# Dilated attention on one core: the two heads of a pair alternate on opposite halves of TensorE, and the next scores stand between transposes and value products

## What is computed

```python
DILATED_GROUPS = ((128, 1), (512, 4), (2048, 16))      # window, dilation; 16 heads of 64 in each

def dilated_attention_mixer(h, w_qkv, q_gain, k_gain, w_o, rel_bias):
    qkv = (h @ w_qkv).reshape(b, s, N_ATTN_GROUPS, 3, HEADS_PER_GROUP, HEAD_DIM)
    for g, (window, dil) in enumerate(DILATED_GROUPS):
        q = head_rms_norm(qkv[:, :, g, 0], q_gain[g])
        k = head_rms_norm(qkv[:, :, g, 1], k_gain[g])
        v = qkv[:, :, g, 2]
        ...
        o, l = dilated_group_attention(q, k, v, bias_g, dil, (window // 2) // dil)
    ...

def dilated_group_attention(q, k, v, bias_g, dil, n_side):
    ...
    sc = jnp.einsum('brnqhe,brnkhe->brnhqk', qb, kb, preferred_element_type=jnp.float32) * (e ** -0.5)
    sc = jnp.where(allowed[None, None, :, None], sc + bias, -1e30)
    m = jnp.max(sc, axis=-1, keepdims=True)
    p = jnp.exp(sc - m)
    den = jnp.sum(p, axis=-1, keepdims=True)
    o = jnp.einsum('brnhqk,brnkhe->brnqhe', (p / den).astype(v.dtype), vb)
```

## Time and profile before

| | |
|---|---|
| median of 3 runs | 3167.93 us (3167.38 to 3170.23) |
| time of the profiled execution | 3171.36 us |
| its span in the trace | 3169.6 us |
| mean granted clock of TensorE | 0.95 of full speed |
| TensorE busy with matmuls | 2895.6 us, 91% |
| the attention stage's three groups, from the first values to the last product | about 1148 to 1785 us of the span |

### The profile page before, as it was taken

One profiled execution on the slowest core, in us unless ns is written; L12 is line 12 of the kernel. 1 busy time (PEld: TensorE's weight loads), 2 busy tenths in 40 slices (PEclk: granted clock), 3 DMA queues, 4 the chain that ended last, 5 costly groups with the idle time before them and its releaser, 6 DMA issues.

```text
span 3169.6 us, 39147 instructions
## 1 busy us (share of the span) xinstructions
PE 2895.6 (91%) x15958; PEld 2352.6 (74%) x15958; DVE 1562.8 (49%) x2318; ACT 1096.0 (35%) x1689; POOL 237.6 (7%) x216
## 2 busy tenths in 40 slices
PE   6999997489999989989999799999799999889877
PEld 5787886467888878768797478888688888566665
DVE  5776663834434434543424554344544343543665
ACT  4332332343222224534525332222332122532442
POOL 2333220010000000000000120000200000010000
PEclk9999998789999989989999899999899999898888
DMA  3244547433443221112231232222122222211101
GB/s 116 88 143 154 161 149 209 188 119 101 133 125 106 94 92 57 67 52 83 69 114 67 94 108 98 93 95 104 42 93 93 98 102 93 76 41 41 39 15 42
DMA packets 115140, 305.40 MB, mean 96 GB/s; under 512 B 28064, under 2 KB 73568, under 8 KB 86160
## 3 DMA queue, kind: packets, MB, share of 16 engines
q1 hardware_dynamic: 109840, 281.41, 27.0%
q10 hardware_dynamic: 5120, 21.50, 1.8%
HBM read 265.20 MB, written 41.85 MB: 97 GB/s over the span
## 4 chain that ended last, share of the span: by engine, by line
PE 80%; DVE 8%; ACT 3%; issue 2%; POOL 1%; SPq 1%; DMA 0%; DVEq 0%; ACTq 0%; POOLq 0%
PE ps L94 78%; DVE s_ L121 2%; PE ps L99 1%; SPq L158 1%; DVE H_ L121 1%; DVE htf_ L135 1%; ACT htf_ L117 1%; ACT wh_ L117 0%; ACT hh_ L117 0%; DVE wl_ L121 0%; DVE Pm_ L121 0%; ACT sq_ L117 0%; DVE ol_ L121 0%; DVE nmx_ L143 0%; DVE R_ L121 0%
## 5 line engine op out<-in xcount | busy, mean ns | idle before, releaser
L94 PE MATMUL ps<-hh_,wh_ 128*128 128x512 f32 x2184 | 874.0, 400 | 23.9 <-DVE hl_ L121 12.7
L94 PE MATMUL ps<-hl_,wh_ 128*128 128x512 f32 x2184 | 857.7, 393 | 0.0
L94 PE MATMUL ps<-hh_,wl_ 128*128 128x512 f32 x2184 | 856.7, 392 | 0.0
L121 DVE TENSOR_TENSOR wl_<-raw_,wh_ 128x2048 fp32r<-128x2048 f32 (+2 forms) x213 | 481.1, 2259 | 543.0 <-ACT wh_ L117 543.0
L117 ACT ACTIVATE wh_<-raw_ 128x2048 fp32r<-128x2048 f32 (+2 forms) x213 | 399.7, 1876 | 341.4 <-PE ps L94 324.8
L94 PEld LDWEIGHTS ps<-hh_,wh_ 128*128 128x128 f32 x2184 | 414.9, 190 | 127.5 <-DVE hl_ L121 11.4
L94 PEld LDWEIGHTS ps<-hl_,wh_ 128*128 128x128 f32 x2184 | 415.0, 190 | 87.3 <-issue 4.0
L94 PEld LDWEIGHTS ps<-hh_,wl_ 128*128 128x128 f32 x2184 | 414.2, 190 | 88.1
L94 PE MATMUL ps<-ah_,wl_ 128*128 128x512 f32 x704 | 279.5, 397 | 0.0
L94 PE MATMUL ps<-ah_,wh_ 128*128 128x512 f32 x704 | 278.3, 395 | 0.0
L94 PE MATMUL ps<-al_,wh_ 128*128 128x512 f32 x704 | 277.8, 395 | 0.0
(11 more groups left out here) (337 smaller groups left out, 3612.7 us busy)
## 6 DMA issues: line engine op xcount, KB each, us to landing
raw_<-in_w SPq DMA_DIRECT2D x205, 1024.0 KB, 4.9
sO<-s5ce_ SPq DMA_DIRECT2D x32, 256.0 KB, 4.0
sW<-s5wt_ SPq DMA_DIRECT2D x16, 512.0 KB, 3.7
sA<-os_ SPq DMA_DIRECT2D x24, 256.0 KB, 2.2
ol_<-sA SPq DMA_DIRECT2D x24, 256.0 KB, 3.9
sT<-sK SPq DMA_DIRECT2D x32, 128.0 KB, 3.3
wh_<-sO ACTq DMA_DIRECT2D x4, 1024.0 KB, 11.6
wl_<-sO ACTq DMA_DIRECT2D x4, 1024.0 KB, 13.2
```

The lines of the kernel that those rows point to most:

```text
L94: return self.e.matmul(out, lhsT, rhs, start=start, stop=stop, skip_group_check=True)
L121: return Nothing() if self.e is None else self.e.tensor_tensor(out, a, b, op)
```

## The change

In `scores_tensor` the loop over the heads becomes the innermost: for each block the matmul of head 0 (SBUF partitions 0 to 63, the upper half of the array's rows) is followed by that of head 1 (partitions 64 to 127). The banks of both heads are waited for before the first of a part. In `products_tensor` the value products alternate likewise between output partitions 0 to 63 and 64 to 127 (the two halves of the array's columns), and wait for the turned tiles of both heads. For that, `turned_parts` lists the parts of both heads next to each other. All transposes of a pair now run in one go; behind them come the scores of the next pair, and then all value products. Step 1 and step 8 keep the order of their pieces.

```diff
--- before.py
+++ after.py
@@ -1590,7 +1590,7 @@
                  (2, 0, 128, 2), (2, 128, 128, 3), (3, 0, 128, 3), (3, 128, 64, 4)]
     else:
         parts = [(x, 0, 128, x) for x in range(4)]
-    return [(h, parts[b:b + 4]) for h in range(2) for b in range(0, len(parts), 4)]
+    return [(h, parts[b:b + 4]) for b in range(0, len(parts), 4) for h in range(2)]
 
 
 def turned_number(g, c, n):
@@ -1676,18 +1676,20 @@
 def scores_tensor(K, pe, g, c):
     q, k = K.att.qk[c % 2]
     w = 256 if g == 0 else 128
-    for h in range(2):
-        r = slice(64 * h, 64 * h + 64)
-        for b0, blocks in enumerate(score_parts(g)):
-            b = K.mb.take("S", g, c, h, b0)
+    pe.wait_ge(*K.at("a.hn", g, c, 0))
+    pe.wait_ge(*K.at("a.hn", g, c, 1))
+    for b0, blocks in enumerate(score_parts(g)):
+        banks = [K.mb.take("S", g, c, h, b0) for h in range(2)]
+        for h in range(2):
             pe.wait_ge(*K.after(pe, K.mb, "S", g, c, h, b0))
-            pe.wait_ge(*K.at("a.hn", g, c, 0))
-            pe.wait_ge(*K.at("a.hn", g, c, 1))
-            for n, x in enumerate(blocks):
-                lo, hi = (max(0, 128 * x - 64), min(512, 128 * x + 192)) if g == 0 else (128 * x, 128 * x + 128)
-                o = w * n + (lo - (128 * x - 64) if g == 0 else 0)
-                m = pe.mm(b[:, o:o + hi - lo], q[r, 128 * x:128 * x + 128], k[r, lo:hi], True, True)
-            m.then_inc(*pe.up("S", g, c, h, b0))
+        for n, x in enumerate(blocks):
+            lo, hi = (max(0, 128 * x - 64), min(512, 128 * x + 192)) if g == 0 else (128 * x, 128 * x + 128)
+            o = w * n + (lo - (128 * x - 64) if g == 0 else 0)
+            for h in range(2):
+                r = slice(64 * h, 64 * h + 64)
+                m = pe.mm(banks[h][:, o:o + hi - lo], q[r, 128 * x:128 * x + 128], k[r, lo:hi], True, True)
+                if x == blocks[-1]:
+                    m.then_inc(*pe.up("S", g, c, h, b0))
     pe.mark("a.S", g, c)
 
 
@@ -1744,7 +1746,7 @@
         ac.mark("a.P", g, c, h)
 
 
-def products_tensor(K, pe, g, c):
+def products_tensor(K, pe, g, c, scores=None):
     A = K.att
     i = c % 2
     O = K.gb.take("O", g, c)
@@ -1752,14 +1754,16 @@
     todo = turned_parts(g)
 
     def weigh(n):
-        h, sub = todo[n]
         t = turned_number(g, c, n)
         pe.wait_ge(*K.at("a.PT", t))
-        hd = 2 * c + h
-        for y, (x, c0, nk, vt) in enumerate(sub):
-            m = pe.mm(O[64 * h:64 * h + 64, 128 * x:128 * x + 128], A.V[0:nk, vt, 64 * hd:64 * hd + 64],
-                      A.PT[t % 4][0:nk, 128 * y:128 * y + 128], g != 0 or y % 2 == 0, g != 0 or y % 2 == 1)
-        m.then_inc(*pe.up("a.w", t))
+        pe.wait_ge(*K.at("a.PT", t + 1))
+        for y, (x, c0, nk, vt) in enumerate(todo[n][1]):
+            for h in range(2):
+                hd = 2 * c + h
+                m = pe.mm(O[64 * h:64 * h + 64, 128 * x:128 * x + 128], A.V[0:nk, vt, 64 * hd:64 * hd + 64],
+                          A.PT[(t + h) % 4][0:nk, 128 * y:128 * y + 128], g != 0 or y % 2 == 0, g != 0 or y % 2 == 1)
+                if y == 3:
+                    m.then_inc(*pe.up("a.w", t + h))
 
     if c == 0:
         for j in (-2, -1):
@@ -1774,10 +1778,10 @@
         m.then_inc(*pe.up("T", t))
         if n == 1 and c + 2 < 8:
             head_tensor(K, pe, g, c + 2, 1)
-        if n > 1:
-            weigh(n - 2)
     pe.mark("a.T", g, c)
-    for n in range(max(0, len(todo) - 2), len(todo)):
+    if scores is not None:
+        scores_tensor(K, pe, g, scores)
+    for n in range(0, len(todo), 2):
         weigh(n)
     pe.mark("O", g, c)
 
@@ -1838,11 +1842,11 @@
             if c == 8:
                 scores_tensor(K, pe, g, 7)
             if c > 1:
-                products_tensor(K, pe, g, c - 2)
+                products_tensor(K, pe, g, c - 2, c - 1 if c < 8 else None)
             if c < 2:
                 head_tensor(K, pe, g, c, 1)
-            if 0 < c < 8:
-                scores_tensor(K, pe, g, c - 1)
+            if c == 1:
+                scores_tensor(K, pe, g, 0)
     pe.mark("end", "pe", "attend")
 
 
```

## The result

| | before | after |
|---|---|---|
| median | 3167.89 us of 4 runs (3167.38 to 3170.23) | 3133.68 us of 4 runs (3130.6 to 3134.51) |
| ratio, with its 95% interval | | 0.9889 (0.9872 to 0.9906) |
| span of the profiled execution | 3169.6 us | 3132.4 us |

The change saves 34.2 us; 3133 was forecast, with 3125 to 3146 as the range. The page of the kernel after still gives most of the chain that ended last to TensorE, 79%; the earlier trace rows had 80%.

The account below looks back on a forecast made before the run. TensorE's sequence between projections was taken as the bound, until another engine's copy is late. Gains of 14.5 + 6.5 + 1.3 + 9.3 + 3.2 = 34.8 us gave 3133 us, range 3125 to 3146.

Parts of the forecast that it names:

- Two heads at the price of one: Scores and value products: alternating heads run at once on the array, so two take the time of one.
- The rival without paired products: Value products keep their length and only the scores gain: 9 us in all, 3159; chance 0.05.
- the one with a fresh start at each change of head: Scores and products: each change of head costs 0.1 or 0.05 us, some 55 us slower, 3223; chance 0.03.
- Steps of groups 1 and 2: Norm sum to projection, steps 2 to 6 of two groups: 5.05 us, gain 1.45 a step, 14.5 us.
- the hole: TensorE's wait: groups 1 and 2, some 0.35 us before scores, for ScalarE's copy; group 0, 1.1 inside scores, for VectorE's.
- Steps of group 0: Norm sum to projection, steps 2 to 6: 9.0 us instead of 10.31, gain 1.3 a step, 6.5 us.
- First scores: Step 1 of each group: 1.64 becomes 1.09 in groups 1 and 2, about 0.2 in group 0; together 1.3 us.
- The end of group 0: Step 7 to group end: VectorE starts pair 6 2.9 earlier and products shorten; gain 9.3 us.
- The ends of groups 1 and 2: Last stretches of both groups: 1.2 to 2.1 us gained, taken as 1.6 each, 3.2 us together.
- The sum: Whole kernel: all gains add to 34.8, say 35 us, giving 3133 us.
- The ends don't move: Group ends held by something else, so only steps and first scores gain: 22 us, 3146; chance 0.09.
- The bank waits aren't there: Scores run right behind the transposes in all groups' steps: 7.5 us more gain, 3125; chance 0.05.

Follow-up runs that it names:

- e1: Kernel before with only the scores alternating between heads; value products and place of the scores as before: 3158.15 us, ratio 0.9971.
- e2: Kernel before with only the value products alternating between heads; scores and their place as before: 3161.36 us, ratio 0.9981.
- e7: Changed kernel with the wait for the bank that comes free last issued first: 3135.61 us, ratio 0.9905.
- the second execution: The changed kernel measured and profiled again without any edit: 3137.59 us, ratio 0.9904.
- e10: Changed kernel with VectorE copying turned tiles before scaling, ScalarE between the norm's two operations, and the later bank's wait first; second measurement: 3127.98 us, ratio 0.9876.
- e4: Changed kernel with scores put back behind the value products, both still alternating: 3151.36 us, ratio 0.9947.
- e6: Changed kernel with scores and products changing heads after two matmuls instead of one: 3148.69 us, ratio 0.9945.
- e3: Kernel before with only the new place, scores between transposes and value products; each head's matmuls stay a block: 3157.39 us, ratio 0.9967.

## Why the prediction was right

**Two heads at the price of one** held for both. e1 has the scores at 1.09 and e2 the products at 1.03, with the other part as before; I had computed 1.08 and 1.02. The rival without paired products is out by e2, the one with a fresh start at each change of head by the 15 and 16 records above. For the Trainium skill's rule (TensorE: Matmul & The Clock Gate, Part 3), by which a load passes running matmuls only on another row group, the measurement decides against it here: the sixteen `PT_,V_` loads use the same rows, and stand in 0.85 us at the full clock, under matmul records that fill 0.84 of the same 0.85. In reading I counted one record too many: 8 start in those 0.71 us and the ninth was already running; the reading stands. That the scores wait for two banks is how the kernel places the heads; no run puts both heads in one bank, so the trace neither bears out nor denies that they must be apart.

**Steps of groups 1 and 2**: 5.15, not 5.05. The owner of the hole was right, ScalarE's first copy; 0.09 of the difference is the second wait, as e7 shows. My working had a slip too: half of 1.92 and half of 0.20 is 1.06, not 1.02, so the terms as I had them give 5.08; the products took 1.02 all the same. 10 x 1.35 is 13.5, for 14.5.

**Steps of group 0**: 9.02 for 9.0, with the hole where it was put, 0.94 us by the row at 1266.41, for 1.1. Five steps are 6.5 us.

**First scores**: 0.13 in group 0 (2.47 to 2.34) and twice 0.55, 1.2, for 1.3.

**The end of group 0**: 10.0 (44.33 to 34.36), for 9.3; the second execution has 9.5. Products 6 start at 19.6 in the stretch (1360.38 - 1340.78) and were at 22.6 (1369.54 - 1346.97), so 3.0 earlier for 2.9. They take 3.6 and those of pair 7 3.7, where I had 4.0 each.

**The ends of groups 1 and 2**: 2.4 each in the first profile (21.8 to 19.4, and in group 2 22.0 to 19.6), for 1.6. That is the term that was mis-sized. Its parts in group 1: products 6 start 1.24 earlier, for 1.1; they take 1.91 instead of 2.81, for 0.9; products 7 start 2.47 after the transposes instead of 1.90, a loss of 0.6 for 0.8, since the transposes ran partly at the full clock; and they take 1.02 instead of 1.87. The last two hang on the clock, and this can't be worked out from the program. The second execution gives 1.2 for group 1, inside my 1.2 to 2.1, and 2.15 for group 2; but it then loses 1.2 in the matmuls for V behind group 1, a term that my sum puts at nothing.

**The sum** of these as measured: 13.5 + 6.5 + 1.2 + 10.0 + 4.8 is 36.0, for 34.8 forecast and 36.4 read from the stretch; another 0.3 comes from the projections of the steps. The misses are 1.1 less and 0.7 + 1.6 more; the forecast's closeness owes something to that. It owes something to the execution as well: beside its own runs of before the change saves 34.2 us in one group of runs and 29.7 in the other, where the median is 3137.6, 4.6 above the forecast and inside the range. The mechanism is borne out step by step; that the time hit 3133 within a microsecond is luck.

**The rivals.** "The ends don't move" is out: they give 14.8 us in the first profile of the kernel after and 12.8 in the second. "The bank waits aren't there" is out for the change, the hole is in each step of group 0. e10 shows what getting rid of them is worth, 9.6 us, where I had computed 7.5; it takes moving the copies on VectorE and ScalarE and turning the order of two waits on TensorE. What I had taken for one cost of the place is two opposite ones: e4 shows that the new place loses 0.4 a step in group 0 and wins 0.9 a step in groups 1 and 2. I had reckoned with the hole, but hadn't compared the places with both alternating.

Not settled: what makes the clock return earlier in one execution of a program than in another.

## What to carry to other kernels

Two independent streams of 64 rows or 64 columns take little more than the time of one when they alternate: 1.64 to 1.10 us for the scores, whose heads met at the seam before, and 1.92 to 1.02 for the products. But alternating also binds the start of both to the later of two inputs; put work between the inputs' making and their use, or the gain turns into a wait, as in e2. Look for who releases the PSUM banks: moving the copies on two other engines, with the order of the waits, gave 9.6 us on top of the 29.7 that the change gave beside it. Let shapes of one kind meet, and write the wait that comes last first. And profile a kernel twice before you explain a difference of 3 us in 3130.

## What was not expected of the hardware

- A second wait of a queue that comes behind the one that ends last costs 0.09 us by itself (2.94 against 3.03 from norm sum to scores, e7 against after).
- A change of the rows in use between 64 and 128 costs 0.3 us among alternating products of 0.055 us a record, the pairing lost around it included (e6).
- Two blocks of matmuls on opposite halves pair at their seam by themselves, as soon as the second has no wait: 1.51 us for sixteen products instead of 1.92 (e3).
- The end of group 1 takes 19.4 or 20.7 us in executions of one program, since TensorE goes back from 1.2 to 2.4 GHz ahead of products 7 in one (granted clock 1.00 over them) and not in the other (0.50), after the same sequence of work. The granted clocks of the whole stretch are 0.82 and 0.74, and the late return costs another 1.2 us in the matmuls behind it.
